# A two-layer hybrid decoder step on one core: outer products and spread rows from stacked rounded halves, states as the moving operand, and a projection that shares a place

## The chip, the cores and the metric

One Trainium2 chip, one of its cores. The metric is device time in microseconds (us) of one execution of the program, the median of several runs.

## The reference: what is computed

One inference step of two layers, for a prompt group of 256 tokens and a sample group of 8 requests with one token each. The columns of both groups stand side by side, so that every activation is a matrix of 264 columns. In each layer

```python
h = x @ w_in                        # one projection, columns split among five branches
# A gated DeltaNet, B sparse attention over selected keys, C retention, D RG-LRU, E memory attention
merged = sum_b sigmoid(gate_b(x)) * (branch_b(h) * silu(gate path)) @ w_branch[b]
x = layer_norm(alpha * x + merged @ w_out)
```

For the sample group, branches A (DeltaNet) and C (retention) hold a state S of 128 x 128 for each of 8 requests and 4 heads. One step reads the state with the key and with the query, forms a new value v, and adds an outer product: S <- g S + k v^T, o = g S^T q + (k.q) v. Branches E and B attend, for each request, with its one query over 256 gathered keys.

## The kernel before

**Weights.** A layer is a list of 174 chunks of work (`plan`), numbered here from 0. A chunk is 16 steps of the contraction (the `gate` chunks have 17), and each step is three products, of the rounded high half of the weight with the high and the low half of the activation and of the low half of the weight with the high half of the activation (L609 to L611, 128 x 264, a rounded 32-bit type). ScalarE makes the high halves (L1190), VectorE the low halves (L1459), in four slots, so that at most two chunks are ready ahead. The last step of a `gate` chunk is the projection of a branch output in full 32-bit (L625, four products); VectorE multiplies and adds its result (L1487, or L1489 and L1490).

**The order of the work** is written out by hand on every engine. TensorE's program is the branch work; between its steps it calls `stream(n)`, which runs chunks until n more are complete, or `fill(n)`, which runs n steps ahead of what is planned (a later `stream` has then less to do). `stream` on ScalarE and VectorE does their part of the same chunks, and `ahead` makes the halves of one more chunk. VectorE's small dependent operations are chained: each waits for the one before it.

**One step of the states** (`samples_step`, n = 0 for DeltaNet, 1 for retention, four heads each, so 16 heads in all). For each head TensorE multiplies 8 states, as the stationary operand, with two columns, key and query (L1015); `stream(1)`; VectorE has meanwhile formed the new values (L1909 to L1917, 8 columns each) and scaled the states (L1920); TensorE transposes the values to rows (L1020), `fill(5)`; VectorE spreads the rows over a block-diagonal mask (L1923, 8 x 1024); two outer products in full 32-bit, 8 x 128 by 8 x 512 each (L1024); VectorE adds them to the states (L1926). Behind that, heads of even number run one more `stream(1)`, and `count`/`topk` do one step of a search for the selected keys (L685 on TensorE, L1582 to L1548 on VectorE):

```python
dve.tensor_tensor(S, S, bb[:, 2:4, :]..., ALU.add).then_inc(sem.s_new, 1)
if m < 7:
    topk()                 # ahead(), then one step of the search
if h % 2 == 0:
    stream(1)
```

TensorE does the same two things in the other order (`stream(1)`, then `count`), and the VectorE step waits for `count`.

**Attention of the samples** (`sample_attend`, n = 0 memory, 1 selected keys). The 8 query rows are transposed (`to_rows`, L723), copied to SBUF (L1644) and spread, one request at a time, over all 128 partitions by a full 32-bit product of 8 x 128 by 8 x 512 (L760). VectorE multiplies each with the keys (two of L1650) and reduces (L1654). Two such rows may be ahead of VectorE.

**Places.** `PLACE` puts the 17 projections of a layer into 15 places of SBUF. Scratch (`zarea`, `garea`) lies over places that are free at the time.

Of the kernel before, what the change touches and what calls it, by code (L numbers as in the profile page):

```python
# [24 lines left out]
ALU = mybir.AluOpType  # L25
# [44 lines left out]
PLACE = {GQ: 0, GK: 1, GV: 2, RQ: 3, RK: 4, RV: 5, DQ: 6, DK: 7, DV: 8, DZ: 9, RZ: 10, LZ: 11, IQ: 12, MQ: 13, GZ: 13,  # L70
         MZ: 14, LX: 14}
# [12 lines left out]
def plan():  # L84
# [5 lines left out]
    def gates(n):  # L90
        chunks.extend(("gate", n, m) for m in range(KC))
# [77 lines left out]
def last_stored(l, is_it):  # L169
# [8 lines left out]
    tok_mm=2, kk_mm=1, inv_T=2, at_mm=2, y_mm=12, z_mm=12, u_mm=2, bt_mm=1, pt_mm=2, o_mm=2, qk_mm=2, sk_mm=8,  # L178
# [17 lines left out]
def tables():  # L196
# [80 lines left out]
def trunk(nc, a, o, at, fixed_w):  # L277

    n_pool = a.cache_dsa_k.shape[1]
    with ExitStack() as ctx:  # L280
# [19 lines left out]
        small = sb("small", [P, 1040])  # L300
        pm8 = sb("pm8", [P, 8])
# [33 lines left out]
        memT = area(DV, 0, KC * NMEM).rearrange("p (c n) -> p c n", n=NMEM)  # L335
# [6 lines left out]
        ysrow = area(DV, 0, D)  # L342
# [124 lines left out]
        qrow, lrow = work[0:NB, 1056:1568], work[0:32, 1568:1568 + KS + 1]  # L467
# [15 lines left out]
        in_lo = garea(2560, 2048).rearrange("p (b g x) -> p b g x", b=NB, g=NPG)  # L483
# [41 lines left out]
        with nc.Block() as block:  # L525
# [45 lines left out]
            def _(pe):  # L571
# [103 lines left out]
                for l in range(DEPTH):  # L675
# [327 lines left out]
                    def samples_step(n, kslot, qslot, vslot):  # L1003
# [3 lines left out]
                        mm = to_rows(H(kslot), 1, (NP, T))  # L1007
# [164 lines left out]
            def _(act):  # L1172
# [26 lines left out]
                def stream(n=1):  # L1199


                    for i in islice(chunks, n):
# [25 lines left out]
                        else:  # L1228
                            if (x, m) == (RZ, 0):
# [1032 lines left out]
```

## Time and profile before

| | |
|---|---|
| median of 3 runs | 3084.67 us (3082.45 to 3085.25) |
| the profiled execution | 3083.64 us, of which 3081.8 us lie between first and last instruction |
| mean granted TensorE clock | 0.965 of full |
| TensorE busy | 2923.6 us, 95% |
| VectorE busy | 1693.9 us, 55% |
| ScalarE busy | 970.3 us, 31% |

A product is shown as one record for the rounded type and as two for full 32-bit, and records of TensorE overlap, so that the time of a run of products is read from the start of the first to the start of what follows. Rows of the timeline begin with start and duration in us; what stands in brackets is how long the engine had been idle, and which instruction ended that.

### The profile page before, as it was taken

The page shows a single profiled execution, that of the slowest core. Times are in us where ns is not written, and L with a number is a line of the kernel's source. Part 1 is how long each engine was busy: PE and PEld are TensorE (multiplying, and loading weights), DVE is VectorE, ACT ScalarE, POOL GpSimd, SP SyncE. Part 2 cuts the span into 40 slices and gives each one's busy share as a digit, 9 for nine tenths or more (in the row PEclk, how much of TensorE's full clock was granted, in tenths as well). Part 3 has the DMA queues.
Part 4 walks back from the last instruction along what each step waited for, and adds up shares of the span by engine and source line. Part 5 has one row for each costly group of instructions (what it writes and reads, how often), then busy time and mean ns, then how long its engine had stood idle before and what let it go on. Part 6 is the DMA issues. An engine that isn't in the chain of part 4 may idle for free.

```text
span 3081.8 us, 49873 instructions
## 1 busy us (share of the span) xinstructions
PE 2923.6 (95%) x21616; PEld 2746.5 (89%) x21616; DVE 1693.9 (55%) x2442; ACT 970.3 (31%) x1299; POOL 184.6 (6%) x209
## 2 busy tenths in 40 slices
PE   8999988999999999999999999799999999999997
PEld 7988888998999898899999788799898998989997
DVE  1464377656566656444434545766666657564444
ACT  1433242223243332333234233322233423322333
POOL 0000000000000003100000100000000000040000
PEclk9989999999999999999999899999899999999998
DMA  6765343465656557666557744444656565576652
GB/s 197 202 176 169 119 126 100 126 160 138 176 152 169 153 155 201 196 172 181 151 149 199 205 137 121 112 113 131 167 147 162 160 176 145 158 211 182 174 155 83
DMA packets 831147, 485.75 MB, mean 158 GB/s; under 512 B 26132, under 2 KB 812820, under 8 KB 829938
## 3 DMA queue, kind: packets, MB, share of 16 engines
q1 hardware_dynamic: 808880, 407.70, 49.0%
q0 software_dynamic: 20448, 68.92, 7.2%
q10 hardware_dynamic: 1600, 5.93, 0.6%
q8 instruction: 171, 2.80, 0.4%
q14 instruction: 48, 0.39, 0.0%
HBM read 466.27 MB, written 16.47 MB: 157 GB/s over the span
## 4 chain that ended last, share of the span: by engine, by line
PE 81%; DVE 14%; ACT 3%; issue 1%; DMA 1%; POOL 0%; DVEq 0%; POOLq 0%; ACTq 0%; SPq 0%
PE mb L609 18%; PE mb L610 18%; PE mb L611 18%; PE mb L625 8%; DVE wsplit L1459 3%; PE mb L596 2%; PE mb L599 2%; DVE work L1817 1%; PE bb L1024 1%; PE bb L863 1%; PE bb L868 1%; PE bb L760 1%; DVE work L1807 1%; PE bb L971 1%; ACT wsplit L1190 1%
## 5 line engine op out<-in xcount | busy, mean ns | idle before, releaser
L609 PE MATMUL mb<-xsplit,wsplit 128*128 128x264 f32 (+1 forms) x5312 | 1584.6, 298 | 35.1 <-DVE wsplit L1459 27.8
L610 PE MATMUL mb<-xsplit,wsplit 128*128 128x264 f32 (+1 forms) x5312 | 1529.0, 288 | 0.0
L611 PE MATMUL mb<-xsplit,wsplit 128*128 128x264 f32 (+1 forms) x5312 | 1527.6, 288 | 0.0
L609 PEld LDWEIGHTS mb<-xsplit,wsplit 128*128 128x128 f32 (+1 forms) x5312 | 1021.5, 192 | 73.2 <-issue 56.4
L610 PEld LDWEIGHTS mb<-xsplit,wsplit 128*128 128x128 f32 (+1 forms) x5312 | 1021.7, 192 | 8.9 <-issue 3.8
L611 PEld LDWEIGHTS mb<-xsplit,wsplit 128*128 128x128 f32 (+1 forms) x5312 | 1015.4, 191 | 1.1
L1459 DVE TENSOR_TENSOR wsplit<-ring,wsplit 128x1024 fp32r<-128x1024 f32 (+2 forms) x664 | 776.7, 1210 | 182.4 <-ACT wsplit L1190 169.2
L1190 ACT ACTIVATE wsplit<-ring 128x1024 fp32r<-128x1024 f32 (+2 forms) x664 | 662.5, 1042 | 137.5 <-PE mb L611 106.2
L1217 ACT ACTIVATE gbuf<-mb 128x264 f32<-128x264 f32 x160 | 62.4, 390 | 838.3 <-PE mb L611 825.5
L625 PE MATMUL mb<-work,bring 128*128 128x264 f32 x1280 | 310.6, 385 | 0.0
L1489 DVE TENSOR_TENSOR gbuf<-gbuf,mb 128x264 f32<-128x264 f32 x128 | 54.9, 429 | 431.9 <-PE mb L625 424.3
L625 PEld LDWEIGHTS mb<-work,bring 128*128 128x128 f32 x1280 | 231.4, 189 | 31.6
L1231 ACT ACTIVATE work<-mb 128x264 f32<-128x264 f32 x136 | 52.8, 389 | 575.3 <-PE mb L611 575.3
L1493 DVE SCALAR_TENSOR_TENSOR work<-work,mb 128x264 f32<-128x264 f32 x32 | 13.7, 429 | 103.9 <-PE mb L611 103.9
L596 PE MATMUL mb<-work,ring 128*128 128x256 f32 x256 | 60.3, 386 | 0.6 <-DVE work L1505 0.6
L1764 DVE SCALAR_TENSOR_TENSOR work<-bb,mws 128x1024 f32<-128x1024 f32 x16 | 19.6, 1225 | 73.9 <-PE bb L863 73.9
L1490 DVE TENSOR_TENSOR merged<-merged,gbuf 128x264 f32<-128x264 f32 x128 | 55.5, 433 | 4.5
L599 PEld LDWEIGHTS mb<-ring,work 128*128 128x128 f32 x512 | 57.5, 192 | 0.1
L599 PE MATMUL mb<-ring,work 128*128 128x128 f32 x512 | 57.5, 275 | 0.0
L2139 POOL DMA_INDIRECT work<-in_cache_dsa_k_dram,rowsU x32 | 38.0, 1188 | 312.5 <-DVE rowsU L2073 302.1
L596 PEld LDWEIGHTS mb<-work,ring 128*128 128x128 f32 x256 | 47.3, 190 | 6.8 <-DVE work L1505 0.7
L760 PE MATMUL bb<-work,tab 8*128 8x512 f32 x64 | 40.2, 738 | 10.5 <-DVE work L1650 10.5
(444 smaller groups left out, 2246.4 us busy)
## 6 DMA issues: line engine op xcount, KB each, us to landing
ring<-in_w_in_dram SPq DMA_DIRECT2D x592, 512.0 KB, 4.8
bring<-in_w_branch_dram SPq DMA_DIRECT2D x160, 256.0 KB, 3.1
ring<-in_w_out_dram SPq DMA_DIRECT2D x64, 512.0 KB, 4.6
ring<-in_w_mem_kv_dram SPq DMA_DIRECT2D x32, 512.0 KB, 3.8
work<-in_cache_mem_k_dram POOLq DMA_DIRECT2D x16, 512.0 KB, 5.4
work<-in_cache_mem_v_dram POOLq DMA_DIRECT2D x16, 512.0 KB, 4.2
work<-in_state_gdn_dram POOLq DMA_DIRECT2D x8, 512.0 KB, 5.3
out_s_gdn_dram<-work POOLq DMA_DIRECT2D x8, 512.0 KB, 4.5
```

The lines of the kernel that those rows point to most:

```text
L596: mm = pe.matmul(bank[:, 0:NMEM], w, memT[:, q, :], start=first, stop=last)
L599: mm = pe.matmul(bank[:, t * P:(t + 1) * P], memT[:, q, t * P:(t + 1) * P], w, start=(first and t == 0), stop=last, skip_group_check=True)
L609: pe.matmul(bank[0:n, 0:T], wh, ah, start=first, stop=False)
L610: pe.matmul(bank[0:n, 0:T], wh, al, start=False, stop=False)
L611: mm = pe.matmul(bank[0:n, 0:T], wl, ah, start=False, stop=last)
L625: mm = pe.matmul(mb[:, (g + 1) % 4, 0:T], bring[:, j % 2, q, :], y[:, q, :], start=(q == 0), stop=(q == CPS - 1))
L760: pe.matmul(bb[:, b % 2, :], id8[:, b:b + 1].to_broadcast([NB, P]), qrow, start=True, stop=True)\
L1190: act.activation(hi(wsplit[:, s % 4, 0, :, 0:n]), ring[:, p % NRING, :, 0:n], ACT.Copy)\
L1217: act.activation(gbuf[:, :], src[:, 0:T], ACT.Sigmoid).then_inc(sem.gate_act, 1)
L1459: dve.tensor_tensor(hi(wsplit[:, s % 4, 1, :, 0:n]), ring[:, p % NRING, :, 0:n], wsplit[:, s % 4, 0, :, 0:n], ALU.subtract).then_inc(sem.l ...
L1489: v(dve.tensor_tensor(gbuf[:, :], gbuf[:, :], proj, ALU.mult))
L1490: dve.tensor_tensor(merged[:, m, :], merged[:, m, :], gbuf[:, :], ALU.add).then_inc(sem.merged_ok, 1)
```

## The change

Four edits. (1) The outer products and the spread query rows are made in the rounded type: each value is split into a high and a low part, and the parts are stacked as rows. For the outer product 24 rows (high, high, low of the key against high, low, high of the value), the first half of the requests on partitions 0 to 23 and the second on 32 to 55; for the query 16 rows (high, low). (2) The states are no longer the stationary operand: 32 columns of keys and queries are, on four column groups in turn, and the states stream past them. The result has keys and queries as rows, so VectorE copies it to SBUF and TensorE transposes it back. (3) `DQ` shares the place of `RQ` and is projected after four chunks of `gates(1)`; `RK` takes its old position. ScalarE waits for `yc_ok` (branch C done) before it stores `DQ`. (4) The buffer `rounded` takes the space that is freed; some scratch moves.

```diff
-PLACE = {GQ: 0, GK: 1, GV: 2, RQ: 3, RK: 4, RV: 5, DQ: 6, DK: 7, DV: 8, DZ: 9, RZ: 10, LZ: 11, IQ: 12, MQ: 13, GZ: 13,
-         MZ: 14, LX: 14}
+PLACE = {GQ: 0, GK: 1, GV: 2, RQ: 3, DQ: 3, RK: 4, RV: 5, DK: 6, DV: 7, DZ: 8, RZ: 9, LZ: 10, IQ: 11, MQ: 12, GZ: 12,
+         MZ: 13, LX: 13}
...
-    project(MZ, IQ, DQ, RQ, GQ, GK, GV, GZ, RK, RV)
+    project(MZ, IQ, RK, RQ, GQ, GK, GV, GZ, RV)
     gates(0)
     project(LX, RZ, LZ, DK, DV, DZ)
-    for n in range(1, len(BRANCH)):
+    gates(1, 0, 4)
+    project(DQ)
+    gates(1, 4)
+    for n in range(2, len(BRANCH)):
         gates(n)
...
+    rows = np.concatenate([e8] * 3 + [np.zeros((8, 8))])
+    add("halves", np.concatenate([rows[:, 0:4], rows[:, 4:8]])[0:56])
+    add("eye8x2", np.concatenate([e8] * 2))
...
-            return (zarea, garea)[n](2048, 1024, NB)
+            return rounded[0:56, W:2 * W]
...
-            return work[0:NB, 0:W]
+            return rounded[0:56, 0:W]
...
+        qrow = rounded[0:2 * NB, 0:W]
+        def kq32(h, b):
+            c = 512 + 2 * (h * NB + b)
+            return work[:, c:c + 32]
...
-                        to_rows(H(qslot), 0, (NP, T)).then_inc(sem.qr_mm, 1)
+                        pe.wait_ge(sem.qr_ok, base.qr_ok + 2 * n + 1)
+                        to_rows(qhl, 0, (0, 2 * NB)).then_inc(sem.qr_mm, 1)
                         stream(1)
-                        pe.wait_ge(sem.qr_ok, base.qr_ok + n + 1)
+                        pe.wait_ge(sem.qr_ok, base.qr_ok + 2 * n + 2)
...
-                            pe.matmul(bb[:, b % 2, :], id8[:, b:b + 1].to_broadcast([NB, P]), qrow, start=True, stop=True)\
+                            pe.matmul(bb[:, b % 2, :], hi(pick)[:, b:b + 1].to_broadcast([2 * NB, P]), hi(qrow), start=True, stop=True)\
...
-                                mm = pe.matmul(bb[:, 0, 2 * b:2 * b + 2], sbuf(n)[:, h % 2, b, :], kq(n)[:, h, b, :],
+                                p0, c0 = 32 * (b % 4), P * (b // 4)
+                                mm = pe.matmul(bb[p0:p0 + 32, 0, c0:c0 + P], kq32(h, b), sbuf(n)[:, h % 2, b, :],
                                                start=True, stop=True)
                             mm.then_inc(sem.sk_mm, 1)
+                            fill(4)
+                            pe.wait_ge(sem.vn_ok, base.vn_ok + 2 * m + 1)
+                            for j in range(2):
+                                mm = pe.transpose(bb[:, 0, NP + j * P:NP + (j + 1) * P], skrows[:, j * P:(j + 1) * P], ident)
+                            mm.then_inc(sem.sk_mm, 1)
                             stream(1)
-                            pe.wait_ge(sem.vn_ok, base.vn_ok + m + 1)
-                            pe.transpose(bb[0:NB, 1, 0:P], vnew(n)[:, h, :], ident).then_inc(sem.vt_mm, 1)
+                            pe.wait_ge(sem.vn_ok, base.vn_ok + 2 * m + 2)
+                            pe.transpose(bb[0:56, 1, 0:P], vhl, ident).then_inc(sem.vt_mm, 1)
                             fill(5)
...
-                                mm = pe.matmul(bb[:, 2 + j, :], ktok(n)[:, h * P:(h + 1) * P], vmask(n)[:, 512 * j:512 * (j + 1)],
+                                mm = pe.matmul(bb[:, 2 + j, :], hi(ktok(n))[32 * j:32 * j + 24, h * P:(h + 1) * P], hi(vmask(n))[32 * j:32 * j + 24, :],
...
-                            if (x, m) == (RZ, 0):
+                            if (x, m) == (DQ, 0):
+                                act.wait_ge(sem.yc_ok, K[l].yc_ok + 1)
+                            if (x, m) == (DK, 0):
                                 act.wait_ge(sem.s_out, K[l].s_out + 16 * NH)
...
+                        q = H((MQ, DQ)[n])[:, :, NP:T]
+                        v(dve.tensor_copy(hi(qhl[:, :, 0:NB]), q))
+                        dve.tensor_tensor(hi(qhl[:, :, NB:2 * NB]), q, qhl[:, :, 0:NB], ALU.subtract).then_inc(sem.qr_ok, 1)
...
+                        for j in (0, 8, 32, 40):
+                            v(dve.tensor_copy(hi(khl[:, :, j:j + NB]), ks))
+                        for j in (16, 48):
+                            v(dve.tensor_tensor(hi(khl[:, :, j:j + NB]), ks, khl[:, :, 0:NB], ALU.subtract))
...
-                            dve.wait_ge(sem.sk_mm, base.sk_mm + m + 1)
+                            dve.wait_ge(sem.sk_mm, base.sk_mm + 2 * m + 1)
+                            dve.tensor_copy(skrows, bb[:, 0, 0:2 * P]).then_inc(sem.vn_ok, 1)
+                            dve.wait_ge(sem.sk_mm, base.sk_mm + 2 * m + 2)
...
+                            for j in (0, 16, 32, 48):
+                                v(dve.tensor_copy(hi(vhl[:, j:j + NB]), vnew(n)[:, h, :]))
+                            v(dve.tensor_tensor(hi(vhl[:, 8:16]), vnew(n)[:, h, :], vhl[:, 0:NB], ALU.subtract))
+                            dve.tensor_tensor(hi(vhl[:, 40:48]), vnew(n)[:, h, :], vhl[:, 0:NB], ALU.subtract).then_inc(sem.vn_ok, 1)
+                            dve.wait_ge(sem.vn_ok, base.vn_ok + 2 * m + 2)
...
-                            dve.tensor_tensor(vmask(n).rearrange("p (b e) -> p b e", b=NB), bh(bb[0:NB, 1, 0:P], NB), bc(id8, P), ALU.mult)\
+                            dve.tensor_tensor(hi(vmask(n)).rearrange("p (b e) -> p b e", b=4), bh(bb[0:56, 1, 0:P], 4),
+                                              bc(tb("halves")[0:56, :], P), ALU.mult)\
```

## Rows read from the trace of the kernel before

**Rows 1.** The page: busy time and share of TensorE; the chain that ended last.

```profile
PE 2923.6 (95%) x21616; PEld 2746.5 (89%) x21616; DVE 1693.9 (55%) x2442; ACT 970.3 (31%) x1299; POOL 184.6 (6%) x209
...
PE 81%; DVE 14%; ACT 3%; issue 1%; DMA 1%; POOL 0%; DVEq 0%; POOLq 0%; ACTq 0%; SPq 0%
```

**Rows 2.** Groups by line: busy us, mean ns, idle before; two records a product.

```profile
L760 PE MATMUL bb<-work,tab 8*128 8x512 f32 x64 | 40.2, 738 | 10.5 <-DVE work L1650 10.5
...
L1024 PE MATMUL bb<-work 8*128 8x512 f32 x64 | 31.7, 613 | 1.9 <-DVE work L1923 1.7
```

**Rows 3.** Timeline of VectorE, DeltaNet heads 1 to 2, layer 0.

```profile
685.28 1.22 DVE L1926 TENSOR_TENSOR work<-work,bb 128x1024 f32<-128x1024 f32 x1 [2.07 <-PE bb L1024]
686.42 2.35 DVE L1459 TENSOR_TENSOR wsplit<-ring,wsplit 128x1024 fp32r<-128x1024 f32 x2
688.69 0.22 DVE L1582 TENSOR_SCALAR small<-bb,small 128x7 f32<-128x7 f32 x1
...
692.05 0.15 DVE L1909 TENSOR_TENSOR work<-bb,small 128x8 f32<-128x8 f32 x1
692.24 0.17 DVE L1910 TENSOR_TENSOR work<-work 128x8 f32<-128x8 f32 x1
```

**Rows 4.** Timeline of TensorE, the same stretch.

```profile
685.41 1.93 PE L1015 MATMUL bb<-work 128*128 128x2 f32 x16
...
690.25 0.42 PE L609 MATMUL mb<-xsplit,wsplit 128*128 128x264 f32 x1
690.47 0.42 PE L610 MATMUL mb<-xsplit,wsplit 128*128 128x264 f32 x1
...
693.43 0.29 PE L610 MATMUL mb<-xsplit,wsplit 128*128 128x264 f32 x1
693.55 0.29 PE L611 MATMUL mb<-xsplit,wsplit 128*128 128x264 f32 x1
...
695.77 1.98 PE L1024 MATMUL bb<-work 8*128 8x512 f32 x4 [0.85 <-DVE work L1923]
```

**Rows 5.** Timeline of TensorE's chain: 8 transposes, one record each.

```profile
302.63 1.82 PE bb L858 x8
```

**Rows 6.** Timeline of TensorE: 8 products on column groups of 32.

```profile
249.52 0.65 PE L789 MATMUL bb<-work 128*32 128x128 f32 x16 [0.78 <-DMA work<-in_cache_mem_v_dram]
```

**Rows 7.** Timeline of TensorE: a long idle time, then 4 products of 128x264.

```profile
721.26 3.86 PE L900 MATMUL bb<-work,tab 128*128 128x264 f32 x8 [5.82 <-DVE small L1558]
```

**Rows 8.** Timeline of TensorE: one gate projection, chunk 66.

```profile
644.09 1.94 PE L625 MATMUL mb<-work,bring 128*128 128x264 f32 x8
```

**Rows 9.** Timeline of TensorE: key norm and token rows (chunks 50 and 51).

```profile
453.98 3.86 PE L900 MATMUL bb<-work,tab 128*128 128x264 f32 x8 [5.73 <-ACT work L1324]
467.22 3.34 PE L723 MATMUL bb<-tab,work 128*128 128x128 f32 x16 [2.61 <-DVE work L1818]
```

**Rows 10.** Timeline, memory attention of the samples, first four requests.

```profile
196.36 1.98 PE L760 MATMUL bb<-work,tab 8*128 8x512 f32 x4
...
197.51 1.28 DVE L1650 TENSOR_TENSOR work<-work,bb 128x512 f32<-128x512 f32 x2 [3.56 <-PE bb L760]
...
200.09 1.28 DVE L1650 TENSOR_TENSOR work<-work,bb 128x512 f32<-128x512 f32 x2
...
201.43 2.07 PE L760 MATMUL bb<-work,tab 8*128 8x512 f32 x2 [1.45 <-DVE work L1650]
...
211.15 1.12 PE L760 MATMUL bb<-work,tab 8*128 8x512 f32 x2
```

**Rows 11.** Timeline, start of the selected-key attention.

```profile
1194.58 0.60 PE L723 MATMUL bb<-tab,work 128*8 128x128 f32 x4
...
1195.32 0.46 DVE L1490 TENSOR_TENSOR merged<-merged,gbuf 128x264 f32<-128x264 f32 x1
```

**Rows 12.** Timeline of TensorE, end of retention (chunks 90 to 92).

```profile
869.98 0.56 PE L609 MATMUL mb<-xsplit,wsplit 128*128 128x264 f32 x1 [3.03 <-DVE wsplit L1459]
```

**Rows 13.** Timeline of VectorE, the same stretch.

```profile
873.16 1.25 DVE L1970 TENSOR_TENSOR work<-work 128x1056 f32<-128x1056 f32 x1
```

More of the change, by code:

```diff
@@ L88, in project, with gates @@
         chunks.extend(("in", s, m) for s in slots for m in range(CPS))
-    def gates(n):
-        chunks.extend(("gate", n, m) for m in range(KC))
+    def gates(n, m0=0, m1=KC):
+        chunks.extend(("gate", n, m) for m in range(m0, m1))
     chunks.extend(("mem", 0, m) for m in range(2 * CPS))
@@ L177 @@
     gt_mm=1, rot_mm=5, ki_mm=1, qd_mm=1, new_mm=1, ik_T=8, ik_mm=8, ik_sc=8, tk_mm=19, gc_mm=1, tails=4, ss=4,
-    tok_mm=2, kk_mm=1, inv_T=2, at_mm=2, y_mm=12, z_mm=12, u_mm=2, bt_mm=1, pt_mm=2, o_mm=2, qk_mm=2, sk_mm=8,
+    tok_mm=2, kk_mm=1, inv_T=2, at_mm=2, y_mm=12, z_mm=12, u_mm=2, bt_mm=1, pt_mm=2, o_mm=2, qk_mm=2, sk_mm=16,
     vt_mm=8, op_mm=8, mean_mm=1, lru_mm=2, h_mm=1, pidx_mm=2, ln_sum=1, ln_ss=4, params_in=192, tab_in=16, mem_in=16,
@@ L181 @@
     lru_act=2, lru_a=1, lru_c=1, pidx_rel=2, mh_ok=4, ln_sq=4, ln_rs=1, xh_ok=16, param_cols=1, memT_ok=8,
-    pages_ok=1, rows_copied=9, lg_ok=4, pr_ok=4, y_e=4, qr_ok=2, kv_used=16, lx_ok=2, lt_ok=2, lp_ok=2, lpt_ok=4,
+    pages_ok=1, rows_copied=9, lg_ok=4, pr_ok=4, y_e=4, qr_ok=4, kv_used=16, lx_ok=2, lt_ok=2, lp_ok=2, lpt_ok=4,
     sy_ok=2, small_a=1, small_c=1, small_e=1, gt_ok=1, rot_ok=5, ki_ok=1, qd_ok=1, new_ok=1, ik_rel=8, sc_ok=8,
     dt_raw=1, tk_ok=18, tails_ok=4, conv_done=4, normed=4, tok_ok=2, kk_ok=2, inv_at=2, lvl_bt=12, z_ok=12, u_ok=2,
-    bt_ok=1, pt_ok=2, st_ok=2, kq_ok=2, qk_ok=2, vn_ok=8, vm_ok=8, s_new=8, mean_ok=1, yc_ok=1, lru_b=1, lru_o=1,
+    bt_ok=1, pt_ok=2, st_ok=2, kq_ok=2, qk_ok=2, vn_ok=16, vm_ok=8, s_new=8, mean_ok=1, yc_ok=1, lru_b=1, lru_o=1,
     h_rows=1, pidx_acc=2, rows_ok=1, ms_ok=4, ln_cen=4, ln_x=16, x_ok=16, rows_out=176, memv_out=16, tail_out=128,
@@ L300, in trunk @@
         small = sb("small", [P, 1040])
+        rounded = sb("rounded", [P, 2 * W + NB])
         pm8 = sb("pm8", [P, 8])
@@ L334, in trunk @@
         memrow = area(RK, 0, 2 * D).rearrange("p (t n) -> p t n", t=2)
-        memT = area(DV, 0, KC * NMEM).rearrange("p (c n) -> p c n", n=NMEM)
+        memT = area(DZ, 0, KC * NMEM).rearrange("p (c n) -> p c n", n=NMEM)
         xrow = area(GQ, 0, 2 * D).rearrange("p (t n) -> p t n", t=2)
@@ L341, in trunk @@
         yrow = area(RK, 0, 2 * D).rearrange("p (t n) -> p t n", t=2)
-        ysrow = area(DV, 0, D)
+        ysrow = area(DZ, 0, D)
         def hi(ap):
@@ L378, in trunk @@
         nsel, nsc = sm(1, NB), sm(1, NB)
+        pick = rounded[0:2 * NB, 2 * W:2 * W + NB]
         sgn, kth, num, need, eoff, foff = (sm(1) for _ in range(6))
@@ L447, in vnew @@
             return work[:, 608:640].rearrange("p (h b) -> p h b", h=NH)
+        khl = work[:, 688:912].rearrange("p (h x) -> p h x", h=NH)
+        vhl = work[:, 912:968]
+        skrows = work[:, 1056:1312]
         qkb = work[:, 640:672].rearrange("p (h b) -> p h b", h=NH)
@@ L466, in trunk @@
         prodK = work[:, 0:1024].rearrange("p (t h d) -> p t h d", t=2, h=NH)
-        qrow, lrow = work[0:NB, 1056:1568], work[0:32, 1568:1568 + KS + 1]
+        qhl = work[:, 0:64].rearrange("p (h x) -> p h x", h=NH)
+        lrow = work[0:32, 1568:1568 + KS + 1]
         maskrow = garea(2048, KS + 1, NB)
@@ L482, in trunk @@
         in_hi = garea(0, 2048).rearrange("p (g b x) -> p g b x", b=NB, g=NPG)
-        in_lo = garea(2560, 2048).rearrange("p (b g x) -> p b g x", b=NB, g=NPG)
+        in_lo = area(RK, 0, 2048).rearrange("p (b g x) -> p b g x", b=NB, g=NPG)
         KI = sb("KI", [P, T])
@@ L1006, in samples_step @@
                         pe.matmul(bb[:, 0, 0:NH * NB], ones, prod(n), start=True, stop=True)
-                        mm = to_rows(H(kslot), 1, (NP, T))
+                        mm = to_rows(khl, 1, (0, 56))
                         mm.then_inc(sem.qk_mm, 1)
@@ L1518, in _ @@
                 dve.wait_ge(sem.tables, 16)
+                v(dve.tensor_copy(hi(pick), tb("eye8x2")[0:2 * NB, :]))
                 for l in range(DEPTH):
@@ L1643, in sample_attend @@
                             v(dve.tensor_tensor(kvprod.rearrange("p (b h) -> p h b", b=NB), H(DK)[:, :, NP:T], H(DQ)[:, :, NP:T], ALU.mult))
-                        dve.tensor_copy(qrow, bb[0:NB, 0, :]).then_inc(sem.qr_ok, 1)
+                        dve.tensor_copy(hi(qrow), bb[0:2 * NB, 0, :]).then_inc(sem.qr_ok, 1)
                         stream(1)
@@ L1899, in samples_step @@
                         v(dve.tensor_copy(qkb.rearrange("p h b -> p (h b)"), bb[:, 0, 0:NH * NB]))
-                        dve.tensor_copy(ktok(n), bb[0:NB, 1, :]).then_inc(sem.qk_ok, 1)
+                        dve.tensor_copy(hi(ktok(n)), bb[0:56, 1, :]).then_inc(sem.qk_ok, 1)
                         stream(1)
@@ L1905, in samples_step @@
                             eg = gam[:, h, :]
[L1906 to L1907 removed]
+                            dve.wait_ge(sem.sk_mm, base.sk_mm + 2 * m + 1)
+                            dve.tensor_copy(skrows, bb[:, 0, 0:2 * P]).then_inc(sem.vn_ok, 1)
+                            dve.wait_ge(sem.sk_mm, base.sk_mm + 2 * m + 2)
+                            sk = bb[:, 0, NP:2 * NP].rearrange("p (b x) -> p b x", x=32)
                             if n == 0:
```

6 lines of the change are left out of this document (2 added, 4 removed).

## Prediction

> **What bounds the kernel now.** I read the page first: TensorE is busy for 95% of the span and 81% of the chain that ended last is its own [rows 1]. So what leaves TensorE shortens the kernel, unless a wait for another engine takes its place; and since everything it does not wait for is filled with weight steps, the question is where it waits. Next the groups by line, for the products that the change touches: 64 records of L1024 in 31.7 us and of L760 in 40.2 us [rows 2], that is 2.0 us for the two outer products of each of 16 heads and 1.26 us for each of 32 spread query rows. Then the timeline, stage by stage. It shows three things. In the heads TensorE hardly ever waits: the one wait is 0.85 us [rows 4]. VectorE, however, is busy from one outer product almost to the next in some heads: between DeltaNet heads 1 and 2 it adds the state at 685.28, splits two weight halves, does a search step from 688.69 and reaches the first operation that reads the product with the states only at 692.05 [rows 3], while TensorE had finished that product at 687.3 [rows 4] and went on with a whole chunk. And TensorE runs at two speeds: neighbouring weight products start 0.12 us apart (2.4 GHz) at 693.43 and 0.22 us apart (1.2 GHz) at 690.25 [rows 4].
>
> **Step 1: the products of a head.** The outer products go from 1.91 us (685.28 less the 2.07 that VectorE waited, to its start) [rows 3] to two rounded ones of 512 columns: at 0.12 us for 264 [rows 4] these take 0.23 us each, 0.47 together, so 1.44 less. The states as stationary operand take 1.93 us [rows 4]. As moving operand against 32 columns, in four column groups in turn, the nearest row is the same shape of product elsewhere, 8 of them in 0.65 us [rows 6]: 1.28 less. If the groups did not overlap it would stay near 1.9. Two transposes are added, at 1.82 us for 8 [rows 5] 0.45 us. Together 2.27 us a head, 9.1 for four heads, 36 us in all 16.
>
> On the outer products a rule bears that no row of before shows. The Trainium skill ("TensorE: Matmul & The Clock Gate", section "Why this matters for your kernels") says that products with few rows that lie in different row groups run at the same time. The change puts its two halves on partitions 0 and 32, so by it the pair would take 0.23 us and the sum would be 16 x 0.23 = 3.7 us lower.
>
> **Step 2: the new round trip.** The copy of the product with the states is queued on VectorE behind the state's add, the splits and the search step; TensorE has only `fill(4)`, 12 products or 1.45 us, before it waits for that copy, where before it had a whole chunk. The copy itself is some 0.43 us (half of the 128 x 1024 add, less a fixed part). I went through the heads with the durations of rows 3.
>
> DeltaNet head 0: VectorE is free, no wait. Head 1: the search step starts with `count`, just before the product, and takes 3.36 us (688.69 to 692.05 [rows 3]); with the copy 3.8, against 0.3 + 0.65 + 1.45 on TensorE: a wait of 1.65 from where it starts. Head 2 follows an odd head, with no chunk between: from the end of the outer product VectorE needs 6.8 (685.28 to 692.05 [rows 3]) and the copy, 7.3 us; TensorE needs 2.4: a wait of 4.85. Head 3: its search step has one threshold for seven, no wait worth counting. The wait of 0.85 [rows 4] goes. In retention the search steps are short (I put 1.8, 1.2 and 0.3 us from their fewer columns): waits of 0.4, 2.65 and 0.
>
> The values: six more chained operations a head, 0.2 us each (692.05 to 692.24 [rows 3]), 1.2 us, hidden by the chunk behind the second product, which at 12 steps is still 4.35 us; what is late then is the mask, and that is cheaper (512 columns for 1024). I count 1.1 us of waits for it in DeltaNet, heads 0 and 1. The six operations on the keys are once a stage, under a whole chunk: nothing; without that chunk they would cost 1.2.
>
> The clock: after an idle time of 5.82 us, 4 products took 3.86 us instead of 2.0 [rows 7], and the weight steps behind them were slow for another 1.1: 3.0 us for a fall. The wait of 4.85 will cost one. But the chunk at 690 already ran slow [rows 4], with no wait ahead of it, only products of two columns; that lost 1.7 us. So 1.3 more.
>
> **Step 3: gate chunks move.** From `RV` on, chunks come four places earlier. Chunks 66 to 69 (the state product's stream, the key rows, head 0 and its end) lose their gate projection, 1.8 us each [rows 8]: 7.2 us. Chunks 50 to 53 get one. At 50 and 51 TensorE idles 5.73 and 2.61 us behind a reciprocal [rows 9], which swallows it whole. At 52 it costs 1.8, at 53 something between 0 and 1.8 (a wait for VectorE may be there); I take 0.7. So 2.5 us early on.
>
> DeltaNet stage: 9.1 + 7.2 - 1.65 - 4.85 + 0.85 - 1.3 - 1.1 = 8.2 us. Retention: 9.1 - 0.4 - 2.65 = 6.0.
>
> At 90 to 92 gates replace plain chunks, at 94 to 97 `DQ` replaces gates: no difference in the sum. But a gate needs VectorE's low halves no more often and lasts longer, so it fills the wait of 3.03 us for them [rows 12]; against it, VectorE now merges three gates, the last for 0.9 us, before it can multiply `RZ` (1.25 us [rows 13]), and TensorE waits for that product: 2.2 us. Net 0.8 won, between 2.2 lost and 4 won. The wait of ScalarE for `yc_ok` costs nothing, as TensorE passes the same wait before it starts the `DQ` chunks that ScalarE would store; were it not so, its splits would stop behind it.
>
> **Step 4: spread query rows.** Memory attention is bound by VectorE: 2.57 us a request (197.51 to 200.09 [rows 10]). TensorE's saving counts only where VectorE waited for it, at the first row of each four, and behind the last: VectorE starts 0.3 us behind TensorE instead of 1.15, needs 4 x 2.57 + 2.36 for the splits, so 13.0 a cycle for the 14.8 of before (196.36 to 211.15 [rows 10]). Twice 1.75: 3.5 us. In the selected-key attention the first four gain about 0.9 (VectorE is still merging a gate), the two pairs behind, where TensorE sets the pace, 1.2 each: 3.3. But `to_rows` now waits for two operations that VectorE does behind the merge ending at 1195.8 [rows 11], at 1196.2 in place of 1194.58 [rows 11]: 1.5 lost. Net 1.8. In the memory attention VectorE is idle at that point: nothing.
>
> **Sum.** Per layer -2.5 + 8.2 + 6.0 + 0.8 + 3.5 + 1.8 = 17.8 us, 35.6 for two. The profiled execution took 3083.6, so 3048.0; the median of the runs is 1.0 above it: 3049. Bounds per layer: lowest gain 4.7 (both chunks paid in full, a second fall of the clock in DeltaNet and one in retention, half of the attention's gains, 2.2 lost at `RZ`), highest 31 (no falls, and the slow chunks of before gone): 3075 to 3022.
>
> **Rivals.**
> - *VectorE takes it all*: where it is busy without pause [rows 3], what TensorE saves becomes waits, and only gates that move into idle time are won, 4.6 us a layer: 3075. For it: VectorE's chain grows by a copy and six operations a head. Against: VectorE waited 2.07 us for the outer product there.
> - *Everything is kept*: TensorE stays at full clock because it streams 128 columns where it had two: 3022. Against it: the wait of 4.85.
> - *Four groups don't overlap*: the product with the states stays at 1.9, 16 x 1.28 = 20 us less: 3069. Against it: [rows 6].
> - *The clock falls at every new wait*, and it ends slower. Place: the 8 heads, the query rows and `RZ`, 10 a layer. Price: 3.0 us each [rows 7]. The forecast has one a layer; 18 more are 54 us: 3103. It decides from 12 more. For it: the outer products keep TensorE busy for a quarter of the time, and [rows 4] shows a fall without a wait. Against: the 0.85 us wait was followed by products at full speed, and there is a chunk of weight steps between any two waits. The Trainium skill ("TensorE: Matmul & The Clock Gate", "Part 1: The HAM clock gate") says that the slow clock is the default and that only sustained activity lifts it; by that rule, shorter products are a risk in themselves. The slow start at 690 agrees [rows 4].
>
> **Numbers.** Chances: forecast 0.52 (its own range 3032 to 3064), VectorE takes it 0.17, everything kept 0.13, no overlap 0.06, clock 0.12. Under 0.2% (6 us, up to 3078.5) this kernel's runs can't tell from no change. Faster: 0.52 + 0.13 + 0.06 and half of the second, 0.80; the other half, 0.08, is the same; slower 0.12. The range 3022 to 3079 takes in all but the clock's case and some tails.
>
> **What would show it.** Right: 8 products with states in about 0.65 us, a pair of outer products under 0.5; TensorE idle some 5 us in DeltaNet head 2 ahead of the two transposes, released by the copy; idle before L900 at chunk 51 still near 4, with a gate projection ahead of it; `to_rows` of the second attention idle for 1.5. Wrong: a granted clock well below 0.965, waits for the copy in most heads, or a total of waits for VectorE that grew by more than 30 us.

## The result, and the profile after

| | before | after |
|---|---|---|
| median of 4 runs | 3083.56 us (3082.19 to 3085.25) | 3032.20 us (3030.77 to 3033.05) |
| profiled execution, span | 3083.64, 3081.8 us | 3032.80, 3031.0 us |
| mean granted TensorE clock | 0.965 | 0.973 |
| TensorE / VectorE busy | 2923.6 / 1693.9 us | 2847.6 / 1713.7 us |

The ratio is 0.9833, interval 0.9821 to 0.9845: 1.7% faster. The forecast was 35.6 us less in the profile; the trace shows 50.8 (3081.8 less 3031.0). The same instruction, looked up in both traces at six places, shows where it came from (us won in each stretch):

| stretch | forecast | layer 0 | layer 1 |
|---|---|---|---|
| to the values' product of the memory attention [rows 6] | 3.5 | 3.4 | 2.8 |
| from there to chunk 66 (gates at 50 to 53) | -2.5 | 4.4 | -2.4 |
| DeltaNet samples, chunks 66 to 73 | 8.2 | 9.1 | 9.1 |
| retention samples | 6.0 | 8.3 | 8.3 |
| chunks 90 to the selected-key attention | 0.8 | 1.5 | 1.9 |
| selected-key attention | 1.8 | 1.6 | 2.8 |
| sum | 17.8 | 28.3 | 22.5 |

The groups by line of the changed kernel (busy us, mean ns, idle before) answer to [rows 2]. The first is the spread query row, then the product with the states, the outer product and the transposes that bring the former back:

```profile
L779 PE MATMUL bb<-rounded 16*128 16x512 f32 x32 | 14.9, 516 | 20.3 <-DVE work L1681 20.3
L1035 PE MATMUL bb<-work 128*32 128x128 f32 x256 | 10.3, 279 | 0.0
L1049 PE MATMUL bb<-rounded 24*128 24x512 f32 x32 | 7.9, 492 | 0.0
L1041 PE MATMUL bb<-tab,work 128*128 128x128 f32 x32 | 7.2, 308 | 18.1 <-DVE work L1942 17.7
```

The products are as cheap as they were forecast, and the last line has the price: 18.1 us of waits that were not there before. The timeline of TensorE at DeltaNet head 2 answers to [rows 4] (L1049 outer, L703 `count`, L1035 states, L627 to L629 weight steps):

```profile
668.55 0.49 PE L1049 MATMUL bb<-rounded 24*128 24x512 f32 x2
668.98 0.39 PE L703 MATMUL bb<-small,memkv 128*128 128x7 f32 x2
669.29 0.64 PE L1035 MATMUL bb<-work 128*32 128x128 f32 x16
669.87 0.40 PE L627 MATMUL mb<-xsplit,wsplit 128*128 128x264 f32 x1
...
676.33 0.69 PE L1041 MATMUL bb<-tab,work 128*128 128x128 f32 x2 [4.74 <-DVE work L1942]
676.67 0.57 PE L627 MATMUL mb<-xsplit,wsplit 128*128 128x264 f32 x1
677.03 0.42 PE L628 MATMUL mb<-xsplit,wsplit 128*128 128x264 f32 x1
677.25 0.42 PE L629 MATMUL mb<-xsplit,wsplit 128*128 128x264 f32 x1
```

From start to what follows, two outer products take 0.43 us and eight products with states 0.58. Then come 12 products, a wait of 4.74, and behind it weight products 0.22 us apart. VectorE in the same stretch answers to [rows 3]:

```profile
669.09 1.22 DVE L1968 TENSOR_TENSOR work<-work,bb 128x1024 f32<-128x1024 f32 x1 [0.93 <-PE bb L1049]
670.23 2.35 DVE L1486 TENSOR_TENSOR wsplit<-ring,wsplit 128x1024 fp32r<-128x1024 f32 x2
672.50 0.22 DVE L1610 TENSOR_SCALAR small<-bb,small 128x7 f32<-128x7 f32 x1
...
675.86 0.41 DVE L1942 COPY work<-bb 128x256 f32<-128x256 f32 x1
677.05 0.17 DVE L1946 TENSOR_TENSOR work<-bb,small 128x8 f32<-128x8 f32 x1 [0.78 <-PE bb L1041]
```

The copy stands where it was expected, behind add, splits and search step, and starts the moment they end. In DeltaNet head 1 and retention head 2 the same line waits 1.66 and 2.47, with weight products at 0.12 us behind both:

```profile
661.03 0.44 PE L1041 MATMUL bb<-tab,work 128*128 128x128 f32 x2 [1.66 <-DVE work L1942]
...
801.79 0.44 PE L1041 MATMUL bb<-tab,work 128*128 128x128 f32 x2 [2.47 <-DVE work L1942]
```

Instead of the waits for the mask that were expected, TensorE waits behind three of DeltaNet's new-value transposes for VectorE's low halves, 0.62 to 0.64 us each (0.7 in all in retention):

```profile
649.46 0.27 PE L1045 MATMUL bb<-tab,work 128*56 128x128 f32 x1
650.35 0.36 PE L627 MATMUL mb<-xsplit,wsplit 128*128 128x264 f32 x1 [0.62 <-DVE wsplit L1486]
```

The clock of retention's heads is what the forecast had not counted. One line of the windows each, the kernel before and then the changed one (start and end, length, busy us of PE, PEld, DVE, ACT, POOL; then the granted clock, DMA share, GB/s):

```profile
783.00:848.00 65.00, 63.69 (x454) 57.83 (x453) 37.20 (x55) 18.26 (x24) 4.68 (x6) 0.95 0.66 173
```

```profile
766.00:822.50 56.50, 51.91 (x454) 48.02 (x453) 40.61 (x83) 18.28 (x24) 4.44 (x5) 1.00 0.74 194
```

Before, two runs of weight products in that stage, some 30 in all, stood 0.22 us apart, at 1.2 GHz, which costs about 3 us; after, no such run is left there. The first run begins so, with TensorE never idle ahead of it in the stage:

```profile
807.91 0.33 PE L611 MATMUL mb<-xsplit,wsplit 128*128 128x264 f32 x1
808.04 0.42 PE L609 MATMUL mb<-xsplit,wsplit 128*128 128x264 f32 x1
808.26 0.42 PE L610 MATMUL mb<-xsplit,wsplit 128*128 128x264 f32 x1
```

The early gates answer to [rows 9]: with gate projections (L643) at chunks 50 and 51 the idle times of 5.73 and 2.61 are 3.93 and 1.12, and the token rows, 3.34 us before, take 1.97. At chunk 52 the gate stands in full:

```profile
446.86 2.10 PE L919 MATMUL bb<-work,tab 128*128 128x264 f32 x4 [3.93 <-ACT work L1351]
...
460.10 1.97 PE L741 MATMUL bb<-tab,work 128*128 128x128 f32 x16 [1.12 <-DVE work L1849]
...
467.70 1.94 PE L643 MATMUL mb<-work,bring 128*128 128x264 f32 x8
```

The first memory requests answer to [rows 10]. VectorE starts 0.5 us behind TensorE, and the cycle of four is 13.5 us (195.92 to 209.40) for 14.8; at the selected keys `to_rows` waits 1.50, as forecast [rows 11]:

```profile
195.92 0.72 PE L779 MATMUL bb<-rounded 16*128 16x512 f32 x2
...
209.40 0.72 PE L779 MATMUL bb<-rounded 16*128 16x512 f32 x2
...
1169.52 0.60 PE L741 MATMUL bb<-tab,work 128*16 128x128 f32 x4 [1.50 <-DVE work L1671]
```

### The profile page after: what moved, and what is told of

The parts are those of the page before. It is cut to its first block and busy times, and to the rows that moved or that the text cites. A ratio compares the mean times of both kernels' runs of the same rounds, so it can differ in the third digit from the quotient of the medians.

```text
span 3031.0 us, 49959 instructions
## 1 busy us (share of the span) xinstructions
PE 2847.6 (94%) x21584; PEld 2696.5 (89%) x21584; DVE 1713.7 (57%) x2587; ACT 975.2 (32%) x1303; POOL 185.6 (6%) x209
## 5 line engine op out<-in xcount | busy, mean ns | idle before, releaser
L627 PE MATMUL mb<-xsplit,wsplit 128*128 128x264 f32 (+1 forms) x5312 | 1579.3, 297 | 34.7 <-DVE wsplit L1486 27.5
L629 PE MATMUL mb<-xsplit,wsplit 128*128 128x264 f32 (+1 forms) x5312 | 1522.0, 287 | 0.0
L627 PEld LDWEIGHTS mb<-xsplit,wsplit 128*128 128x128 f32 (+1 forms) x5312 | 1015.9, 191 | 66.8 <-issue 45.6
L629 PEld LDWEIGHTS mb<-xsplit,wsplit 128*128 128x128 f32 (+1 forms) x5312 | 1010.5, 190 | 1.1
L643 PE MATMUL mb<-work,bring 128*128 128x264 f32 x1280 | 310.6, 385 | 0.0
L643 PEld LDWEIGHTS mb<-work,bring 128*128 128x128 f32 x1280 | 231.3, 189 | 31.6
L1517 DVE TENSOR_TENSOR merged<-merged,gbuf 128x264 f32<-128x264 f32 x128 | 55.5, 433 | 4.4
L1848 DVE RECIPROCAL work<-work 128x1056 f32<-128x1056 f32 x6 | 40.5, 6751 | 15.9 <-ACT work L1357 15.9
```

Of the source, the lines that this page charges most:

```text
L627: pe.matmul(bank[0:n, 0:T], wh, ah, start=first, stop=False)
L629: mm = pe.matmul(bank[0:n, 0:T], wl, ah, start=False, stop=last)
L643: mm = pe.matmul(mb[:, (g + 1) % 4, 0:T], bring[:, j % 2, q, :], y[:, q, :], start=(q == 0), stop=(q == CPS - 1))
L1517: dve.tensor_tensor(merged[:, m, :], merged[:, m, :], gbuf[:, :], ALU.add).then_inc(sem.merged_ok, 1)
```

## The experiments

The total of a kernel moves by a few us for reasons far from an edit: between the end of retention in layer 0 and DeltaNet in layer 1 the changed kernel took 1309.9 us in one execution and 1313.4 in another (E5). So small edits are read in two stages, each from the first product with states to the last outer product, in the profiled execution. The two layers agree within 0.4 us in most kernels:

| kernel | DeltaNet, layers 0 / 1 | retention, 0 / 1 | median | ratio to before (95%) |
|---|---|---|---|---|
| before | 61.1 / 61.1 | 56.8 / 56.8 | | |
| changed (E5) | 55.6 / 55.4 | 48.5 / 48.5 | 3032.7 | 0.9832 (0.9819 to 0.9846) |
| E1 plan only | 57.4 / 56.5 | 56.8 / 55.3 | 3068.7 | 0.9949 (0.9936 to 0.9963) |
| E2 outer full | 58.3 / 58.4 | 54.6 / 54.6 | 3056.9 | 0.9919 (0.9906 to 0.9931) |
| E3 states stationary | 51.5 / 51.5 | 49.3 / 52.4 | 3029.0 | 0.9825 (0.9812 to 0.9838) |
| E4 query full | 55.5 / 55.6 | 48.5 / 48.8 | 3048.7 | 0.9887 (0.9872 to 0.9903) |
| E6 copy on ScalarE | 53.6 / 53.6 | 48.4 / 48.4 | 3032.0 | 0.9827 (0.9813 to 0.9840) |
| E7 copy first | 55.4 / 55.7 | 47.6 / 47.6 | 3038.4 | 0.9846 (0.9832 to 0.9859) |
| E8 casts merged | 53.8 / 53.8 | 48.6 / 48.6 | 3037.7 | 0.9840 (0.9826 to 0.9854) |
| E9 hybrid | 49.8 / 49.9 | 45.0 / 45.2 | 3015.2 | 0.9784 (0.9765 to 0.9804) |
| E10 stationary, casts | 49.9 / 49.9 | 49.7 / 50.8 | 3026.5 | 0.9814 (0.9798 to 0.9830) |
| E11 ScalarE, casts | 49.5 / 49.4 | 46.1 / 46.1 | 3018.8 (one run) | |
| E12 group pairs | 55.4 / 55.6 | 48.5 / 48.5 | 3033.5 (one run) | |

**E1, the plan alone.** The kernel before with the new `PLACE`, `plan`, ScalarE's wait, and scratch moved to fit.

```diff
-    project(MZ, IQ, DQ, RQ, GQ, GK, GV, GZ, RK, RV)
+    project(MZ, IQ, RK, RQ, GQ, GK, GV, GZ, RV)
...
+    gates(1, 0, 4)
+    project(DQ)
+    gates(1, 4)
```

> The kernel before with the new places and the new order of projections and gates alone, all products as before. Theory A (the four parts add up, each where TensorE sets the pace): chunks 66 to 69 lose 4 x 1.8 us a layer, the gates at chunks 52 and 53 cost between 0 and 1.8, the end of retention wins about 1: 6.4 to 8.2 us a layer, so 3067 to 3071. Rival B (in the heads VectorE sets the pace, so that a gate taken out of them becomes a wait): at most 2 us a layer, 3079 or above. A says further that TensorE's idle time in DeltaNet's heads stays under 2 us.

Measured 3068.7, theory A. The DeltaNet stage, which holds two of the four gates, got 3.7 us shorter in layer 0 and 4.6 in layer 1 (where one of the two slow stretches went as well), for the 3.6 that two gates take. TensorE idles 0.87 us in that stage in layer 0 and nothing in layer 1. So the gates come off in full, and VectorE did not set the pace there while the products were long.

**E2, outer products in full 32-bit.** Key rows, mask and new values as before, all else as changed.

```diff
...
-mm = pe.matmul(bb[:, 2 + j, :], hi(ktok(n))[32 * j:32 * j + 24, h * P:(h + 1) * P], hi(vmask(n))[32 * j:32 * j + 24, :],
+mm = pe.matmul(bb[:, 2 + j, :], ktok(n)[:, h * P:(h + 1) * P], vmask(n)[:, 512 * j:512 * (j + 1)],
...
```

> The changed kernel with the outer products in full 32-bit again (8 x 1024 mask, no high and low copies of keys and values), all else as changed. Theory A: 16 x 1.5 us come back, 24 us, so 3056. For the clock two theories: C1, the products of two columns made it fall, and they are gone here too: the granted clock in retention's heads stays at 1.00 and the time is 3056. C2, the long outer products made it fall: the clock in retention's heads goes back to 0.95 and some 3 to 4 us a layer more come back: 3062 to 3065. Rival B: VectorE sets the pace and has 1.2 us a head less to do without the copies, so that only half comes back: 3044.

Measured 3056.9, 24.2 above E5, which is theory A's total. By stages it holds for retention, 6.1 us longer for four times 1.5. DeltaNet is only 2.8 longer: there VectorE, with a shorter chain, takes 1.9 us (layer 0) and 3.3 (layer 1) off TensorE's idle time, which is rival B in part. The stages give 17.9 in all; the other 6 lie outside them, and their cause stays open. The clock follows neither C1 nor C2: the window of retention's heads shows 0.97, between the two.

```profile
773.00:834.00 61.00, 57.10 (x447) 49.83 (x445) 38.22 (x58) 16.98 (x23) 4.44 (x5) 0.97 0.68 181
```

The slow weight products of that window begin right behind the wait for the copy at head 2:

```profile
809.26 0.48 PE L1041 MATMUL bb<-tab,work 128*128 128x128 f32 x2 [2.46 <-DVE work L1938]
809.45 0.52 PE L627 MATMUL mb<-xsplit,wsplit 128*128 128x264 f32 x1
809.76 0.42 PE L628 MATMUL mb<-xsplit,wsplit 128*128 128x264 f32 x1
```

**E3, states stationary.** The product of [rows 4] again, without copy and transposes.

```diff
-mm = pe.matmul(bb[p0:p0 + 32, 0, c0:c0 + P], kq32(h, b), sbuf(n)[:, h % 2, b, :],
+mm = pe.matmul(bb[:, 0, 2 * b:2 * b + 2], sbuf(n)[:, h % 2, b, :], kq(n)[:, h, b, :],
...
-fill(4)
-pe.wait_ge(sem.vn_ok, base.vn_ok + 2 * m + 1)
-for j in range(2):
-    mm = pe.transpose(bb[:, 0, NP + j * P:NP + (j + 1) * P], skrows[:, j * P:(j + 1) * P], ident)
```

> The changed kernel with the states as stationary operand against two columns again, so without the copy and the two transposes, all else as changed. Theory A: 16 x (1.36 - 0.2) = 18.6 us come back, and the waits for the copy (1.66, 4.74 and 2.47 us a layer) and the fall of the clock behind the longest (1.9) go, 21.5 us: about 3029, no worse than the changed kernel. With C1 (two columns make the clock fall) 3 to 5 us a layer more: 3035 to 3039, the granted clock in retention's heads back at 0.95. Rival: the states as moving operand are what pays, 3050.

Measured 3029.0: taken by itself, the second edit buys nothing that the total can tell. The stages say why: DeltaNet is 4.0 us shorter without it, retention 0.8 and 3.9 longer. Retention's clock is 0.97 in layer 0 and 0.91 in layer 1, where some 44 weight products run slow. TensorE is idle in neither, as the line of layer 0 shows. So with products of two columns the clock falls without any wait ahead. For the long outer products alone that is not shown: E2's fall has a wait ahead of it, and E8 below has the same fall behind the same wait with neither kind of product.

```profile
760.00:818.00 58.00, 58.00 (x467) 56.78 (x465) 39.46 (x80) 17.65 (x24) 4.44 (x5) 0.97 0.76 200
```

**E4, query rows in full 32-bit.**

```diff
...
-pe.matmul(bb[:, b % 2, :], hi(pick)[:, b:b + 1].to_broadcast([2 * NB, P]), hi(qrow), start=True, stop=True)
+pe.matmul(bb[:, b % 2, :], id8[:, b:b + 1].to_broadcast([NB, P]), qrow, start=True, stop=True)
...
```

> The changed kernel with the spread query rows in full 32-bit again and no high and low copies of the query, all else as changed. Theory A: 3.5 us of the memory attention and 1.6 of the selected-key attention come back in each layer, 10 us: 3042. Rival: VectorE sets the pace of the attention, so that nothing comes back: 3032 to 3034.

Measured 3048.7, 16.0 above E5. Stage by stage the attentions give back 9.8 us, in sum as theory A has it (memory 2.5 and 2.4 where it had 3.5; selected keys 4.1 less 1.65 of the `to_rows` wait, twice, where it had 1.6). The other 6 lie in stretches that the edit doesn't touch. Every execution of E4 shows a lower granted clock (0.968 to 0.970) than any of E5 (0.971 to 0.973); why stays open.

**E5 to E8, the round trip.** E5 is the changed kernel. E6 gives the copy to ScalarE; E7 leaves it on VectorE, ahead of the search step; E8 merges the small copies of the new values.

```diff
# E6, in ScalarE's program, for each head
...
+ahead()
+act.wait_ge(sem.sk_mm, base.sk_mm + 2 * m + 1)
+act.activation(skrows, bb[:, 0, 0:2 * P], ACT.Copy).then_inc(sem.vn_ok, 1)
+stream(1)
...
# E7, behind the state's add
...
-if m < 7:
-    topk()
+if h == 1:
+    copy_rows(m + 1)
+if m < 7:
+    ahead()
 if h % 2 == 0:
     stream(1)
+    copy_rows(m + 1)
+if m < 7:
+    next(searching)
...
# E8
-for j in (0, 16, 32, 48):
-    v(dve.tensor_copy(hi(vhl[:, j:j + NB]), vnew(n)[:, h, :]))
+v(dve.tensor_copy(hi(vhl4[:, :, 0:NB]), bh(vnew(n)[:, h, :], 4)))
...
```

> The changed kernel unchanged, beside the others of this call on the same chip: 3030 to 3034 by every theory.

> The changed kernel with ScalarE, not VectorE, copying the product with the states. Theory A (what TensorE waits for is the place of the copy in VectorE's queue): the waits of 1.66 and 2.47 us and half of that of 4.74 go, and the slow clock behind the longest with them, 8 us a layer: 3016. Rival B (in the heads VectorE sets the pace anyway): the wait only moves to the new values' rows, the mask or the low halves, and what is won is the copy and its round trip, 1.2 us where there was a wait: 3024 to 3029.

> The changed kernel with VectorE's copy of the product with the states ahead of the search step (and, between odd and even heads, ahead of the splits too); no work less. Theory A: the waits ahead of the transposes go, 8 us a layer as with ScalarE's copy: 3016 to 3020. Rival B (VectorE sets the pace): the transposes no longer wait, but TensorE waits as long behind them, and the time stays at 3029 to 3035.

> The changed kernel with the four high copies of the new values as one instruction and the two low ones as one: four chained VectorE operations of 0.2 us a head less. Theory A (hidden work, priced at nothing in the forecast): the short waits for low halves (0.62 to 0.64 us in three DeltaNet heads, 0.7 in retention) go, some 2.6 us a layer at most: 3027 to 3032. Rival B (VectorE sets the pace of the heads): 0.8 us in most of 16 heads, 3020 to 3022.

E5 came out at 3032.7. None of the other three moved the total as theory A had it, and their totals (3032.0, 3038.4, 3037.7) lie outside rival B's ranges too, so what follows is read from the stages. In E6 and then E7 the transposes at DeltaNet's head 2 no longer wait, but the next transpose, of the new values, does:

```profile
678.36 0.42 PE L1045 MATMUL bb<-tab,work 128*56 128x128 f32 x1 [3.33 <-DVE work L1965]
```

```profile
684.69 0.30 PE L1045 MATMUL bb<-tab,work 128*56 128x128 f32 x1 [3.67 <-DVE work L1958]
```

That is rival B for DeltaNet: from head 1's outer product to head 2's new values VectorE sets the pace, and a wait that is taken away in one place comes back in the next. What takes work off VectorE shortens the stage (E6 and E8, 1.9 and 1.7 us); what only reorders it does not (E7, 55.4 us of 55.6), though in retention E7's order won 0.9. In E8 the waits for low halves are gone and the copy's waits stay at 1.66 and 4.74.

E8's retention stage is no shorter than the changed kernel's (48.6 for 48.5), because a wait that has no slow products behind it there has some 15 behind it here, in both layers:

```profile
798.19 0.44 PE L1042 MATMUL bb<-tab,work 128*128 128x128 f32 x2 [2.46 <-DVE work L1943]
...
762.00:819.00 57.00, 53.92 (x464) 50.71 (x462) 37.17 (x67) 18.28 (x24) 4.44 (x5) 0.97 0.74 195
```

The medians of E7 and E8 are 5 us above E5 although their stages are no longer. All their executions show a lower granted clock (0.966 to 0.970) than any of E5 (0.971 to 0.973), so more of the rest ran slow; why stays open.

**E9 to E11, put together.** E9: stationary in DeltaNet, moving with the copy first in retention, casts merged. E10 is E3 with E8. E11 is E6 with E8.

```diff
# E9
...
+if n == 0:
+    mm = pe.matmul(bb[:, 0, 2 * b:2 * b + 2], sbuf(n)[:, h % 2, b, :], kq(n)[:, h, b, :],
+                   start=True, stop=True)
+else:
+    mm = pe.matmul(bb[p0:p0 + 32, 0, c0:c0 + P], kq32(h, b), sbuf(n)[:, h % 2, b, :],
+                   start=True, stop=True)
...
```

> States stationary in DeltaNet (as before), moving in retention with the copy ahead of the search step, and the merged high and low copies of the new values in both. From the profiles so far the stage of DeltaNet's heads (first product with states to last outer product) takes 51.5 us with stationary states and 55.5 with moving ones, that of retention 47.6 with the copy first and 48.5 without. If these add up: 51.5 or less and 47.6 or less, 5 us a layer below the changed kernel, so 3021 to 3024. Rival (the clock takes it back elsewhere): both stages as short, but the total within 4 us of 3032.

> States stationary in both branches, and the merged copies of the new values. If VectorE sets the pace in DeltaNet's heads even with stationary states, the stage falls from 51.5 by what the merge takes off VectorE, 0.8 us a head or some 2 us in all; if TensorE does, it stays at 51. Retention 49 to 52 as with stationary states. Total 3024 to 3030.

> The changed kernel with ScalarE's copy and the merged copies together. Alone they took the DeltaNet stage from 55.5 us to 53.6 and 53.8. If VectorE sets the pace there, the two add up: 51.8 to 52.3. If each only removes the same wait, it stays at 53.5. Looked at in the stage alone.

E9 is 3015.2 and beats the changed kernel by 17.5 us of the medians, with intervals of the ratio that don't meet (0.9765 to 0.9804, 0.9819 to 0.9846). That is more than the 8 to 11 that were expected: both stages came out shorter than expected, retention 45.0 for 47.6, as the merged copies count there too (E11's retention is 2.3 us shorter than E6's). E10's DeltaNet stage fell by 1.6 us through the merge, so VectorE counts there even with stationary states. In E11 the two edits won 6.1 us of the DeltaNet stage together where they won 1.9 and 1.7 alone; neither expectation had that. TensorE's idle time in the stage is 4.3 us in E11, for 8.3 in the changed kernel, 6.8 in E6 and 6.4 in E8: 4.0 less, where the two alone took off 1.5 and 1.9. Most of the rest is the clock. Alone each kept a slow stretch behind the longest wait (E6 13 weight products from 678.8, E8 22 from 674.4); together the longest wait is 2.55 us, no slow stretch follows it, and the window of DeltaNet's heads shows a clock of 1.00, for 0.94 in the changed kernel. E11 is one execution, and in E8 a wait of 2.46 was followed by a fall, so whether E11 keeps that clock is not shown:

```profile
642.00:692.50 50.50, 45.92 (x400) 42.04 (x398) 38.65 (x80) 18.62 (x26) 4.44 (x5) 1.00 0.75 193
```

```profile
642.00:698.50 56.50, 48.15 (x402) 44.23 (x400) 42.60 (x100) 17.40 (x22) 4.44 (x5) 0.94 0.66 172
```

**E12, order of the column groups.**

```diff
-for b in range(NB):
+for b in (0, 4, 1, 5, 2, 6, 3, 7):
```

> The changed kernel with the eight products of the moving states issued in the order 0, 4, 1, 5, 2, 6, 3, 7, so that neighbours use the same column group. If products on different column groups overlap, this order takes longer than the 0.57 us of the changed kernel, 0.9 us or more from the first to what follows; if they don't overlap and 0.57 is just eight short products, it stays at 0.57.

From 643.66 to 644.25 it is 0.59 us, for 0.58:

```profile
643.66 0.66 PE L1035 MATMUL bb<-work 128*32 128x128 f32 x16
644.25 0.39 PE L627 MATMUL mb<-xsplit,wsplit 128*128 128x264 f32 x1
```

The order of the groups doesn't matter. The expectation would conclude that the groups don't overlap, but the single records behind the merged row show that they do. These lines count (in brackets) the records of L1035, of 16 in all, two a product, that had started 0.13 and 0.23 us after the first, in the changed kernel and then in E12:

```profile
669.29:669.42 0.13, 0.13 (x4) 0.13 (x8) 1.00 1.21 355
669.29:669.52 0.23, 0.23 (x8) 0.23 (x12) 1.00 1.13 316
```

```profile
643.65:643.78 0.13, 0.12 (x4) 0.12 (x8) 1.00 1.20 288
643.65:643.88 0.23, 0.22 (x8) 0.23 (x12) 1.00 1.21 289
```

The records start in fours, one four 0.11 us behind the other, in either order. The eight records of a gate projection [rows 8] take 1.78 us from their start to what follows (644.09 to 645.87), 0.22 us each for 264 columns, so one of 128 columns takes 0.11 (an estimate), and 16 one after the other would take 1.7. So the four column groups work at the same time, the rival "four groups don't overlap" is out, and what was wrong was the test: the order in which the products are issued does not tell.

## Why the forecast was right, and where its size was off

The measured 3032.2 lies at the edge of the forecast's own range (3032 to 3064), 17 us from the forecast and 10 from the rival "everything is kept". What tells the two apart is the wait of 4.74 with its slow stretch, which came as forecast. The mechanism held but for the clock, and part of the total was luck.

**The products of a head**: right. 0.43 and 0.58 us stood for 0.47 and 0.65, the transposes take 0.13 to 0.2 for 0.45 (0.34 at the slow clock). The product of before takes 1.79 from its start to what follows (685.41 to 687.20), not 1.93, which is the length of its row. The plan (E1) gives 14.3 us; E2 gives the outer products 17.9 in the two stages and 24 in the total. The Trainium skill ("TensorE: Matmul & The Clock Gate", section "Why this matters for your kernels") would have the pair on two row groups run at once. The trace agrees as to the start, since in all 16 pairs the second record starts 0.003 or 0.004 us behind the first, but not as to the 0.23 us that the prediction worked out by it, since what follows starts 0.43 us after the first. A spread query row, one product of 16 rows and 512 columns, takes 0.32 or 0.33 to what follows, and two on the same rows 0.65:

```profile
1193.74 0.72 PE L779 MATMUL bb<-rounded 16*128 16x512 f32 x2
1194.39 0.39 PE L627 MATMUL mb<-xsplit,wsplit 128*128 128x264 f32 x1
```

So the pair overlaps in part, and the forecast's 0.47, two products one after the other, was near the time but not for its reason.

**The new round trip**: right in mechanism and size for the waits, 1.66, 4.74 and 2.47 for 1.65, 4.85 and 2.65. The copy's 0.41 us for 0.43 is luck: it has 256 of the add's 1024 columns, a quarter and not half. The waits for the mask (1.1) were instead waits for low halves, 1.9 in DeltaNet and 0.7 in retention. Six more chained operations a head were put at nothing; E8, with four fewer, shows that those four cost 1.7 us a layer in DeltaNet, through those low halves, and E11 beside E6 shows 2.3 in retention.

**The clock**: this term failed. In DeltaNet the sum took -1.3, a fall for 3.0 and an old slow chunk that ends for 1.7; in retention it took nothing. In DeltaNet some 30 slow weight products before became 18 after, which is 1.2 us won; in retention some 30 became none, about 3 us won. The slow chunks of before were seen, but their end stood only in the upper bound. E3 shows that products of two columns come with slow stretches without any wait, and E8 that the clock of 1.00 is not sure without them. The rival "clock falls at every new wait" was wrong: of the three waits for the copy only that of 4.74 was followed by a slow stretch. But waits near 2.5 us went both ways: 2.46 (E2 and E8, retention) and 2.48 (E7, DeltaNet) were followed by slow products, 2.47 (changed kernel) and 2.55 (E11) were not. What decides stays open.

**Gate chunks**: right where TensorE pays. In E1 the gate at chunk 52 delays what follows by 1.9 and 1.8 us, and that at 53 next to nothing (a wait of 1.30 took it, so the 0.7 was too much). Layer 1 lost 2.4 up to chunk 66, as forecast; layer 0 won 4.4 there. Of these 6.9 us, 1.4 are the token rows that no longer run slow behind an idle time; most of the rest are slow stretches in chunks that the change doesn't touch (24 slow weight products between 304 and 331 us before, none there after, 16 around 353). Why they moved stays open, and for the forecast they are luck.

**Query rows, `RZ`**: right in mechanism. `to_rows` lost 1.65 for 1.5. The cycle of four requests came out at 13.5 us where the forecast had 13.0, so the two cycles give 2.6 (E4: 2.5 and 2.4) for 3.5; the 3.4 and 2.8 of the table hold something else besides. The product before `RZ` makes TensorE wait 2.23 for 2.2, and the stretch won 1.5 and 1.9 for 0.8.

So the total missed by 15: 4.6 is retention (its clock alone gave about 6), 6.9 the stretch ahead of chunk 66 in layer 0, 1.8 DeltaNet, and the rest small terms. With the measured terms in place of the forecast's, either stage's sum comes out some 1.5 us above what the stage won (an estimate). Part of that is the end of the product ahead of a wait: the transpose at 649.46 is over only after 0.27 us, and then 0.62 of idle time follow, where before the next product started 0.03 us behind it (663.40 and 663.43). So DeltaNet's total is near the forecast because misses of both signs met. "VectorE takes it all" was wrong for the kernel but holds in part in DeltaNet's heads, where the second edit loses 4 us (E3).

## What to carry to other kernels

When a product gets shorter only by sending its result on a round trip through another engine, look at that engine's queue at the place, head by head: the same edit lost 4 us in DeltaNet, where a long search step stands ahead of the copy, and won in retention, where it is short. Where two engines are close, judge an edit by the time of its stage and not by the wait that it removes: moving a wait won nothing in DeltaNet (E7), taking work off VectorE did (E6, E8), and the two together won more than their sum, as a slow stretch went too (E11). Count the slow stretches of the kernel before as a term of the sum: in retention's heads the clock was low without any wait. And look at the single records before calling products serial or parallel; the total of a group does not tell.

## What the runs showed of the hardware

- In retention's heads the granted clock was 0.95 in the kernel before, with long outer products and products of two columns, and 0.97 and 0.91 with the latter alone (E3, layers 0 and 1), although TensorE was never idle there. It was 1.00 in the changed kernel, with neither, although TensorE was idle for 4.6 of 56.5 us; but it was 0.97 in E8, with neither as well.
- Eight products of 128 columns on 32 output rows took 0.58 us in full 32-bit, whatever the order of the column groups; their records start in fours, 0.11 us apart.
- Two rounded products of 24 rows and 512 columns on partitions from 0 and from 32 start 0.003 us apart and take 0.43 us to what follows; two of 16 rows on the same partitions take 0.65.
- Idle times of 2.46 and 2.48 us were followed by weight products at half speed, others of 2.47 and 2.55 were not.
